# One layer of a hybrid trunk on one core: low-rank projections among the modulation's weight slabs, attention's first value projection at the end of the scan, and output products of four tiles between attention's last units

## The reference

```python
sh1, sc1, gt1, sh2, sc2, gt2 = adaln(cond, w_mod, b_mod)        # silu(cond) @ w_mod + b_mod, 6 x 1024
h = rmsnorm(x, norm1_g) * (1 + sc1) + sh1
proj = jnp.einsum('btd,de->bte', h, w_in)
pa = centred_shift(proj[..., :D_A_COLS], mu_prev, mu_next)       # r, k, v, wlo|alo (64+64), glo (128)
qkv = proj[..., D_A_COLS:].reshape(b, t, 3, H_B, N_B)
ya, s_fin = rwkv_mixer(pa, ...)   # tanh(wlo) @ w_up, alo @ a_up, sigmoid(glo) @ g_up, then the scan
yb = attend(q, k, v)              # neighbourhood attention, 8 heads x 64
x = x + gt1 * jnp.einsum('bte,ed->btd', jnp.concatenate([ya, yb], axis=-1), w_out)
h = rmsnorm(x, norm2_g) * (1 + sc2) + sh2
x = x + gt2 * expert_choice_ffn(h, router, e_gate, e_up, e_down)  # 16 experts
```

## Time and profile before

| what | value |
|---|---|
| time of the kernel, median of 3 runs | 3781.8 us (3779.23 to 3781.97) |
| time of the profiled execution | 3779.4 us |
| its span, first to last instruction | 3777.6 us |
| PE busy | 3515.6 us (93%) |
| DVE / ACT / POOL busy | 1228.5 / 669.6 / 178.3 us |
| mean clock granted to TensorE | 0.969 of full speed |

### The profile page before, as it was taken

One profiled execution on the slowest core, in us unless ns is written; L12 is line 12 of the kernel. 1 busy time (PEld: TensorE's weight loads), 2 busy tenths in 40 slices (PEclk: granted clock), 3 DMA queues, 4 the chain that ended last, 5 costly groups with the idle time before them and its releaser, 6 DMA issues.

```text
span 3777.6 us, 81314 instructions
## 1 busy us (share of the span) xinstructions
PE 3515.6 (93%) x36826; PEld 3080.1 (82%) x36826; DVE 1228.5 (33%) x3107; ACT 669.6 (18%) x1659; POOL 178.3 (5%) x137
## 2 busy tenths in 40 slices
PE   5899999999899979649999999999999999999998
PEld 2477695958655544349999999999999999999998
DVE  3376767767534443541111111111111111111113
ACT  2322424242134452200000000000000000000002
POOL 0010101001011100000000000000000100000001
PEclk8899999999999989769999999999999999999999
DMA  8200000000021003159777777777877777777775
GB/s 330 62 16 4 21 4 21 4 9 14 21 81 33 24 22 113 56 218 356 273 270 276 267 276 270 274 269 268 278 277 275 275 274 269 268 277 274 270 263 194
DMA packets 499783, 665.28 MB, mean 176 GB/s; under 512 B 31566, under 2 KB 438374, under 8 KB 496366
## 3 DMA queue, kind: packets, MB, share of 16 engines
q1 hardware_dynamic: 493742, 640.70, 48.1%
q0 software_dynamic: 5520, 19.34, 1.9%
q10 hardware_dynamic: 176, 0.05, 0.0%
HBM read 631.68 MB, written 28.30 MB: 175 GB/s over the span
## 4 chain that ended last, share of the span: by engine, by line
PE 56%; DMA 0%; DVE 0%; issue 0%; ACT 0%; DVEq 0%; POOLq 0%
PE bank L2202 37%; PE bank L2214 18%; PE bank L2160 0%; PE bank L2225 0%; DMA e_xe<-scratch_h2d,idx 0%; PE bank L2171 0%; ACT e_wd L2295 0%; PE bank L2184 0%; DVE e_ye L2369 0%; DVE e_wu L2455 0%; DVE e_wu L2398 0%; DVE e_xe L2444 0%; DVE e_xpT L2339 0%; DVE e_xT L2333 0%; ACT e_yT L2289 0%
## 5 line engine op out<-in xcount | busy, mean ns | idle before, releaser
L2202 PE MATMUL bank<-e_xT,e_wg 128*128 128x144 f32 x5632 | 749.2, 286 | 1.6 <-DVE e_xT L2335 1.6
L2214 PE MATMUL bank<-e_hid,e_wd 128*128 128x144 f32 x5632 | 747.9, 286 | 0.0
L2202 PE MATMUL bank<-e_xT,e_wu 128*128 128x144 f32 x5632 | 747.5, 286 | 0.0
L2202 PEld LDWEIGHTS bank<-e_xT,e_wg 128*128 128x128 f32 x5632 | 715.3, 190 | 2.0 <-DMA e_wd<-in_e_down 2.0
L2202 PEld LDWEIGHTS bank<-e_xT,e_wu 128*128 128x128 f32 x5632 | 713.7, 190 | 0.0
L2214 PEld LDWEIGHTS bank<-e_hid,e_wd 128*128 128x128 f32 x5632 | 711.0, 190 | 0.0
L2345 DVE TENSOR_TENSOR e_tm<-bank,e_sg 128x144 f32<-128x144 f32 x352 | 108.4, 308 | 1793.7 <-ACT e_sg L2281 1793.7
L2281 ACT ACTIVATE e_sg<-bank 128x144 f32<-128x144 f32 x352 | 102.5, 291 | 1938.5 <-PE bank L2202 1938.5
L532 PE MATMUL bank<-hT_x,wblk 128*128 128x512 f32 (+1 forms) x672 | 236.2, 508 | 14.4 <-DMA wblk<-in_w_in 8.4
L532 PEld LDWEIGHTS bank<-hT_x,wblk 128*128 128x128 f32 x672 | 113.7, 197 | 129.5 <-issue 111.5
L727 PE MATMUL bank<-r_TW,r_X 64*64 64x64 f32 x2880 | 167.6, 220 | 4.3 <-DVE r_X L1198 1.3
(11 more groups left out here) (350 smaller groups left out, 3387.1 us busy)
## 6 DMA issues: line engine op xcount, KB each, us to landing
e_wg<-in_e_gate SPq DMA_DIRECT2D x176, 1024.0 KB
e_wu<-in_e_up SPq DMA_DIRECT2D x176, 1024.0 KB
e_wd<-in_e_down SPq DMA_DIRECT2D x176, 1024.0 KB
h_wmod<-in_w_mod SPq DMA_DIRECT2D x24, 1024.0 KB, 18.7
wblk<-in_w_in SPq DMA_DIRECT2D x22, 512.0 KB
h_x<-in_x_sample SPq DMA_DIRECT2D x8, 512.0 KB, 7.3
wo<-in_w_out SPq DMA_DIRECT2D x2, 2048.0 KB, 11.6
o_x<-in_x_sample SPq DMA_DIRECT2D x8, 512.0 KB
```

Of the source, the lines that this page charges most:

```text
L2202: last = nc.tensor.matmul(bank[6 + b % 2][:, j * TOK:(j + 1) * TOK], w[s][:, k, f], xT[e % 2][:, k, :], start=(k == 0), stop=(k == KD - 1))
L2214: last = nc.tensor.matmul(bank[k // PER_BANK][:, c:c + TOK], wd[s][:, b % DUO, k * P:(k + 1) * P], hid[:, b % 2, :], start=(b == 0 and k % ...
```

## The change

1. In `head`, each slab of groups 1 and 2 is followed on PE by three matmuls of a low-rank block (`wlo|alo` in group 1, `glo` in group 2) on one chunk of `K.hT`, into banks 0 to 5. The weights (two of 512 KB, five small ones, and pair 0's key weights of 512 KB ahead of the last two slabs) are loaded in `head`. `lora` is shifted and gets its tanh in `head` too; `glo`'s copy, shift and sigmoid stay in `rwkv`.
2. In `rwkv`, the three value pieces of attention's pair 0 are projected between the steps of the last `finish`. `attention` then starts with six pieces.
3. In `attention`, units 1 to 8 of the last pair each hold one `out_half`: the eight half products of output tiles 0 to 3, in bank 7, copied by ACT to `K.x2` after `heads_out` and `normalised`. `output` computes the products of tiles 4 to 8 alone, ahead of and behind the transposes of tiles 0 to 7.

```diff
@@ head, SP
-                slabs(KD, GROUPS * KD)
+                for i in range(2):
+                    c = (BLK + i) * P
+                    sp.dma_start(K.wblk[i][:, :, :], w_in_v[:, :, c:c + P]).then_inc(wl_in[i], 16)
...
+                slabs(KD, GROUPS * KD - 2)
+                sp.wait_ge(low_ps, 1)
+                sp.dma_start(K.wblk[0][:, :, :], w_in_v[:, :, DA:DA + P]).then_inc(wk_in, 16)
+                slabs(GROUPS * KD - 2, GROUPS * KD)
@@ head, PE: after the four matmuls of a slab
+                        if g:
+                            kc = KORDER[k]
...
+                            if g == 1:
+                                pe.wait_ge(hd_ok if kc < 4 else ha_ok, kc % 4 + 1)
+                            for c, (at, n) in enumerate(PIECES):
+                                last = nc.tensor.matmul(bank[3 * (g - 1) + c][:, 0:n], K.wblk[g - 1][:, kc, :],
+                                                        K.hT[:, kc, at:at + n], start=(k == 0), stop=(k == KD - 1))
@@ rwkv, PE
-                for i in range(2):
-                    pe.wait_ge(w_in[i], 16)
-                    project(i, 3 * i)
-                pe.wait_ge(rawd, 2)
-                pe.wait_ge(lora_ok, 2)
-                pe.wait_ge(sel_ok, 1)
+                pe.wait_ge(rawd, 1)
...
                 finish_first(PAIRS - 1)
+                pe.wait_ge(w_in[0], 16 * (2 * PAIRS))
+                project(0, 3, pieces=[0], chunks=range(0, 6))
                 finish_var(PAIRS - 1)
+                project(0, 3, pieces=[0], chunks=range(6, KD))
+                project(0, 3, pieces=[1])
                 finish_back(PAIRS - 1)
+                project(0, 3, pieces=[2])
@@ attention, PE
+                def out_half(u, chunks):
+                    i, j = divmod(u - 1, 2)
+                    if chunks[0] == 0:
+                        if u == 1:
...
+                        else:
+                            pe.wait_ge(half_ok, u - 1)
...
-                for n in range(9):
+                for n in range(3, 9):
...
+                    elif u:
+                        out_half(u, range(0, 4))
@@ attention, ACT, end of a unit
+                    if p + 1 == PAIRS and u:
+                        i, j = divmod(u - 1, 2)
+                        act.wait_ge(half_ps, u)
+                        nc.scalar.activation(K.x2[:, i, j * 512:(j + 1) * 512], bank[7][:, :], ACT.Copy)\
+                          .then_inc(half_ok, 1)
@@ output, PE
+                BEFORE = {0: (4, 0), 1: (5, 0), 2: (5, 1), 4: (6, 0), 5: (7, 0), 6: (8, 0), 7: (8, 1)}
+                AFTER = {0: (4, 1), 4: (6, 1), 5: (7, 1)}
                 for i in range(TILES):
-                    product(i, 0)
+                    if i in BEFORE:
+                        product(*BEFORE[i])
+                    turned(i)
+                    if i in AFTER:
+                        product(*AFTER[i])
                     if i:
-                        turned(i - 1)
-                    product(i, 1)
-                    if i:
-                        logits(i - 1)
...
+                        affinities(i - 1)
+                    logits(i)
@@ output, DVE
-                    dve.wait_ge(o_ps, i + 1)
+                    if i < AHEAD:
+                        last = V.tensor_tensor(x2[:, i, :], x2[:, i, :], gt1[:, s, :], ALU.mult)
```

More of the change, by code:

```diff
@@ L256, in _ @@
                     for s, at, n in ((0, 0, NS), (1, NS, NP)):
-                        nc.scalar.activation(K.hT[:, k, at:at + n], K.hT[:, k, at:at + n], ACT.Identity,
-                                             scale=K.s1[:, k, s:s + 1], bias=K.modT[:, SH1 * 8 + k, s:s + 1])
+                        last = nc.scalar.activation(K.hT[:, k, at:at + n], K.hT[:, k, at:at + n], ACT.Identity,
+                                                    scale=K.s1[:, k, s:s + 1], bias=K.modT[:, SH1 * 8 + k, s:s + 1])
+                    last.then_inc(ha_ok, 1)
+                act.wait_ge(zero_ok, 1)
+                act.wait_ge(low_ps, 1)
+                for c, (at, m) in enumerate(PIECES):
+                    to = at + SAMPLE if at < NS else PROMPT
+                    last = nc.scalar.activation(K.raw[:, to:to + m], bank[c][:, 0:m], ACT.Copy)
+                last.then_inc(raw_ok, 1)
+                act.wait_ge(shift_ok, 1)
+                nc.scalar.activation(K.lora[0:HN, :], K.lora[0:HN, :], ACT.Tanh).then_inc(tanh_ok, 1)
             @block.vector
@@ L382, in rwkv @@
     ORDER = (1, 0, 2)
-    BLK = 3 * PAIRS
     THIRD, DUP = NT // 3, 16
@@ L391, in rwkv @@
         prow = sb("prow", [HD, TABW])
-        lora = sb("lora", [P, NT])
+        lora, raw, wup, gup = K.lora, K.raw, K.wup, K.gup
         sigg = sb("sigg", [P, NT])
-        wup = [sb(f"wup{d}", [P, P]) for d in range(2)]
-        gup = sb("gup", [P, P])
         pv2 = [sb(f"pairvec{i}", [P, 15]) for i in range(2)]
@@ L1350, in piece_bank @@
         def piece_bank(p, n):
-            return bank[(0, 1, 2, 3, 4, 5, 0, 1, 2)[n]] if p == 0 else bank[7]
+            return bank[(3, 4, 5, 0, 1, 2, 3, 4, 5)[n]] if p == 0 else bank[7]
         def turn_bank(p, u):
@@ L1568, in _ @@
                         piece(p + 1, u, range(4, 6))
+                    elif u:
+                        out_half(u, range(4, 6))
                     turned(U, 1)
@@ L2496, in trunk @@
                 K.scan_keep = K.sb("scan_keep", [P, NT], BF16, ctx=scan)
+                K.raw = K.sb("raw", [P, RAW_WIDTH], ctx=scan)
+                K.lora = K.sb("lora", [P, NT], ctx=scan)
+                K.lc = K.sb("loraconst", [P, 2], ctx=scan)
+                K.wup = [K.sb(f"wup{d}", [P, P], ctx=scan) for d in range(2)]
+                K.gup = K.sb("gup", [P, P], ctx=scan)
                 head(K, A)
```

207 lines of the change are left out of this document (121 added, 86 removed).

## The result

| | before | after |
|---|---|---|
| median | 3780.5 us (3774.4 to 3782.0, 4 runs) | 3737.6 us (3736.2 to 3739.2, 4 runs) |
| span of the profiled execution | 3777.6 us | 3737.4 us |

The ratio is 0.989, with a 95% interval of 0.9873 to 0.9907: some 42 us less.

A forecast was written before the change was run, and what follows sets the result against it. PE was busy 93% of the span, but its waits ahead of the experts were the target. Gains 37.2 + 9.4 - 3.5 = 43.1 us took 3779.4 to 3736.3, forecast 3738 as median, range 3726 to 3749.

The forecast's parts named there:

- Head: `head` and start of `rwkv`: low-rank matmuls between slabs let the gates begin at 99.7 instead of 136.88, gaining 37.2 us.
- The bound with a second fill of 0.14: `head`: each slab pays 0.14 us again on its second array-shape change, ending at PE's last matmul; gain only 34.0 us.
- End of the scan: Last `finish` and attention's start: DVE goes on 6.1 us later, attention loses 15.5 us of pieces; net gain 9.4 us.
- 12.2 with the clock up: Attention's start: if PE keeps its clock over the short barrier, the low-clock start goes too; gain 12.2 us.
- The last pair: Attention's last pair: with a half in units 1 to 8 it takes 95 us instead of 64.5, a loss of 30.5.
- `output`: `output` stage: DVE's chain of at least 10 us a tile decides; 144 us instead of 171.3, a gain of 27.
- Part three as a whole: Attention's last pair and `output` together: a loss of 3.5 us, with bounds of 8 gained and 10 lost.
- (a): `output`: its chain shortens as PE gets free, 45 of the 55 us come back; total 3720; chance 0.08.
- (b): Last pair: ACT copies the half after the next exponentials, 7 units wait 2 us more each; total 3752; chance 0.08.
- (c): `head`: slabs' groups stay at the low clock, 48 us more; total 3786, no change; chance 0.03.
- (d): Attention's last pair stays at the low clock, 8 units lose 92 us; total 3830, slower; chance 0.03.

The follow-up runs named there:

- every second slab: Changed kernel with the low-rank matmuls of two chunks behind each second slab of `head` instead of one chunk behind each: 3734.1 us, ratio 0.9883.
- part 3 alone: Kernel before the change, with only attention's half products in the last pair and the new `output` added: 3780.2 us against 3777.1, ratio 1.0006.
- early-sigmoid kernel: Changed kernel with a one-element sigmoid on ACT in `head`, right behind `lora`'s tanh, to load the table earlier: 3740.2 us, ratio 0.99.
- parts 1 and 2: Changed kernel without the half products in attention's last pair and with `output` as before the change: 3734.0 us, ratio 0.9881.
- the alternating order: Changed kernel with `output`'s tiles in order 0, 4, 1, 5, 2, 6, 3, 7, 8, three halves first, then one per step: 3722.4 us, ratio 0.9856.

## Why the prediction was right, step by step

The forecast of 3738 us with a range of 3726 to 3749 held: 3737.6.

- **Head, 37.2 us forecast, 35.8 measured** (136.88 less 101.08). The slab was put at 3.00 us and takes 3.13. The bound with a second fill of 0.14 was the nearer one; the run with every second slab shows 0.16 for each change of shape. 16 slabs are 2.1 us more, and group 1 began 0.45 later. PE ends at 97.4 and the scan's stage starts at 99.75, 2.3 us behind instead of 3.5, which gives 1.2 back. The DMAs never bound, as said.
- **The gates' clock was missed.** The head was counted as over at the gates; they ran at 0.50 and took 4.21 us. What that costs by the end of the stage is small: in the two kernels with every second slab, whose gates ran at the full clock (2.27 us in the run by itself), the stage took 870.6 and 869.9 us, 2.1 and 2.8 less than the shortest of the others with part 1. The +2.4 of the first table is not all the change's: part 3 alone, with the scan of before, has 872.7 against 871.7 there, and the other kernels with part 1 have 872.7 to 874.0.
- **End of the scan, 9.4 forecast, 12.2 with the clock up; 11.9 measured**, and 10.1 to 10.2 in seven kernels, where the stretch is 54.7 to 54.8 instead of 53.06. Both prices stood in the text, and which one comes is the clock behind the barrier: 1.00 from 990 to 1000 in the changed kernel, 0.83 in the early-sigmoid kernel. The finish itself came as worked out: the variance began 5.1 us behind the mean's end (980.18 and 975.10), forecast 5.2, and DVE's last products (990.72, the row's 1018.04) stand 15.6 us behind it, forecast 15.7. What the forecast did not have is the 1.4 us that every kernel with part 2 loses at the first scores; with them part 2 gives 10.4 to 10.5.
- **The last pair, 95 forecast, 97.7 measured.** Units 1 to 7 take 81.5 us against 81. Unit 0 took 6.63 instead of 5.55, and unit 8 with its tail and the last copy 9.64 instead of 8.8. In five kernels, without the fall of the clock in the first units, the pair takes 94.9.
- **`output`, 144 forecast, 142.9 measured**, with the steps as followed in the two queues (15, 13, 10, 10, 18, 17, 13, 10): 107.3 us against 106. The first `h2` stood 27.4 us behind attention's end, not 30.0: DVE's wait for the loads ended 15.8 us behind it, where it had been 18.4. PE is idle ahead of tiles 3 and 8, as expected. Part three as a whole: a loss of 3.5 forecast, 5.2 measured beside parts 1 and 2 and 1.4 by itself in the trace, 3.1 by the medians.
- **Rivals.** (a) fell: the chain on DVE and ACT is 10.6 us, and part 3 does not pay in this order of tiles. It could have paid, though: the alternating order takes 16.6 us off. (b)'s 2 us more in each unit did not come, since units 1 to 7 took 81.5 us against 81. But the copy does hold PE somewhat: put first, it takes 2.8 us off these units. (c) fell by the clock of 1.00 in `head`. (d) showed only in the first units of the last pair.

The sum, -43.1, stands against -40.2 between the spans and -42.9 between the medians. Its terms are off by +1.4, -2.5, +2.7 and -1.4 us, which leaves -42.9 for them together; the rest is +2.4 in the scan, +1.4 in pairs 0 to 2 and -1.0 behind `output`. That the terms cancel so well is luck. So is the last part of the agreement in the total: the forecast was counted from a median of 3781.8, and the later medians of the kernel before are 3777 to 3778. What was foreseen rightly is the mechanism of each part and, but for the clock's falls, its size.

## What to carry to other kernels

Work moved into the waits of an engine was worth its whole time and more here, where the wait was for a DMA and the engine idled at a low clock: 36 us for 31 us of matmuls, since the waits around them went too. The price was 0.16 us for each change of array shape, which speaks for few large groups rather than many small ones. Before work is moved out of a stage, count what its other chain takes per step: `output` could give 28 of 55 us because some of its steps are set by PE and others by the chain on DVE and ACT. Moving the work alone paid nothing (a loss of 1 to 5 us); evening out the steps behind it gave 16.6. Whether the new order would gain anything without the moved halves was not run. And a wait that is removed gives nothing where the next one ends at the same event, as the table load showed.

## What the runs showed of the hardware

- A change between the 32-column tiles and the full array goes with 0.16 us in this sequence (0.33 us for two of them, on a pair of slabs).
- PE's clock was at 0.50 for `rwkv`'s gates behind waits of 3.67 and of 2.38 us. Behind one of 2.68 us it was at 1.00 for their first 2.0 us and then at 0.50 for 3.4. Behind attention's barrier, a wait of 2.65 to 2.69 us, it is 0.83 or 1.00 in the same stretch of 10 us. The length of the wait does not tell which.
- The same code's stage took 142.9 or 147.8 us (`output`), 94.9 or 97.7 (the last pair), 53.1 or 54.8 (end of the scan to the scores), each time with another clock in one or two stretches. These differences are larger than what several of the edits were worth.
